# Three engines instead of two for the scale and shift of six norms, and a new order of the retention layer on one Trainium2 core

## The reference, cut to what matters

```
def rms_norm(x, g):
    y = xf * lax.rsqrt(jnp.mean(xf * xf, axis=-1, keepdims=True) + EPS)
    return y * g
def modulate(h, shift, scale):
    return h * (1 + scale) + shift
```

```
pv, q, k, v, g = split(h @ w_in)          # 512, 256, 256, 512, 512 wide
q, k = rope(q), rope(k)                   # a rotation inside each pair of channels
o = retention_bidir(q, k, v) with decays  # 4 heads: (q k^T * decay) v, both directions
y_r = rms_norm(o, gn_g) * silu(g)         # per head
y_p = multiscale_pool(pv)                 # windowed mean minus value, @ pool_w, * pool_scale
y = concat(y_p, y_r) @ w_out
```

## Time and profile before

| | us |
|---|---|
| median of three runs | 2321.37 |
| profiled execution, its device time | 2323.1 |
| span of that execution, first to last instruction | 2321.3 |
| PE busy | 2219.7 |
| DVE busy | 789.0 |
| ACT busy | 372.4 |
| POOL busy | 369.9 |

### The profile page before, as it was taken

How to read it: one execution, slowest core, us unless ns; L and a number is a source line. 1 busy time by engine, 2 the same in 40 slices (tenths; PEclk the granted TensorE clock), 3 DMA queues, 4 the chain that set the end, 5 groups by cost and what they waited for, 6 DMA issues and landing times.

```text
span 2321.3 us, 34149 instructions
## 1 busy us (share of the span) xinstructions
PE 2219.7 (96%) x11074; PEld 1272.1 (55%) x11075; DVE 789.0 (34%) x1709; ACT 372.4 (16%) x849; POOL 369.9 (16%) x2342
## 2 busy tenths in 40 slices
PE   6999999999999998999999899999899899999987
PEld 3464458888544677998888633333233233333323
DVE  1133655555560325884115321122121121111212
ACT  3222212111001312220224210010000010000001
POOL 0000020000001101000100033333233333333332
PEclk9999999999999999999999899999999999999999
DMA  9721342222584705557861399899999989989997
GB/s 381 248 74 55 104 133 91 91 91 82 174 269 146 236 1 182 164 165 260 283 211 61 146 382 422 354 423 422 383 397 422 422 357 422 422 358 422 422 422 289
DMA packets 196206, 602.76 MB, mean 260 GB/s; under 512 B 11042, under 2 KB 128034, under 8 KB 146850
## 3 DMA queue, kind: packets, MB, share of 16 engines
q1 hardware_dynamic: 193728, 599.04, 67.4%
q10 hardware_dynamic: 2402, 2.67, 0.4%
HBM read 600.62 MB, written 1.05 MB: 259 GB/s over the span
## 4 chain that ended last, share of the span: by engine, by line
PE 79%; DMA 12%; SPq 4%; DVE 2%; ACT 1%; POOL 1%; issue 1%; POOLq 0%; ACTq 0%; DVEq 0%
PE bank L371 52%; PE bank L964 26%; DMA wring<-in_w_gu 11%; SPq L2269 4%; DMA wring<-in_mod_w 1%; ACT big L1146 1%; POOL hT L2232 1%; DVE wring L1566 1%; PE bank L996 1%; ACT tmp L1146 0%; PE bank L989 0%; DVE big L1566 0%; DVE tmp L1566 0%; PE bank L677 0%; POOL xT L2259 0%
## 5 line engine op out<-in xcount | busy, mean ns | idle before, releaser
L964 PE MATMUL bank<-wring,big 128*64 128x512 f32 x3456 | 772.9, 596 | 41.1 <-DMA wring<-in_w_gu 32.7
L964 PEld LDWEIGHTS bank<-wring,big 128*64 128x64 f32 x3456 | 235.3, 137 | 529.4 <-issue 411.5
L371 PE MATMUL bank<-hT,wring 128*128 128x256 f32 (+2 forms) x1888 | 456.5, 396 | 8.3 <-POOL hT L2232 5.7
L371 PEld LDWEIGHTS bank<-hT,wring 128*128 128x128 f32 x1888 | 322.8, 193 | 125.1 <-issue 93.6
L371 PE MATMUL bank<-big,wring 128*128 128x256 f32 (+1 forms) x1096 | 344.7, 475 | 6.4 <-DVE big L1569 3.6
L2255 POOL COPY big<-hT 128x8 f32 x2240 | 306.7, 199 | 112.1 <-issue 112.1
L371 PEld LDWEIGHTS bank<-big,wring 128*128 128x128 f32 x1096 | 208.6, 191 | 138.9 <-issue 115.7
L371 PE MATMUL bank<-wring 128*128 128x256 f32 (+1 forms) x1408 | 245.9, 327 | 1.2 <-DVE wring L1566 1.1
L371 PEld LDWEIGHTS bank<-wring 128*128 128x128 f32 x1408 | 216.0, 191 | 20.3 <-DVE wring L1566 1.6
L1146 ACT ACTIVATE big<-bank 128x256 f32<-128x256 f32 (+3 forms) x239 | 89.5, 390 | 774.1 <-PE bank L989 385.4
L1569 DVE TENSOR_SCALAR big<-bank 128x512 f32<-128x512 f32 (+1 forms) x74 | 50.2, 678 | 447.2 <-PE bank L964 446.0
(11 more groups left out here) (169 smaller groups left out, 1240.5 us busy)
## 6 DMA issues: line engine op xcount, KB each, us to landing
wring<-in_w_gu SPq DMA_DIRECT2D x256, 1024.0 KB, 18.7
wring<-in_w_down SPq DMA_DIRECT2D x128, 1024.0 KB, 18.4
wring<-in_ffn_w_up SPq DMA_DIRECT2D x44, 1024.0 KB, 5.1
wring<-in_mod_w SPq DMA_DIRECT2D x24, 1024.0 KB, 15.5
wring<-in_mod_w SPq DMA_DIRECT2D x48, 512.0 KB, 4.4
wring<-in_ffn_w_down SPq DMA_DIRECT2D x16, 1024.0 KB, 5.6
wring<-in_w_ada SPq DMA_DIRECT2D x16, 1024.0 KB, 5.5
wring<-in_w_in SPq DMA_DIRECT2D x14, 1024.0 KB, 11.8
```

Source lines behind the costliest of these rows:

```text
L371: ins = pe.matmul(o, l, r, start=start, stop=stop, skip_group_check=True)
L964: ins = pe.matmul(o, l, r, start=start, stop=stop, skip_group_check=True)
```

## The change

It has two parts, which touch no weight, shape or result. First, the scale and shift of chunks 3 and 7 move from POOL to DVE in every norm: DVE scales chunks 0 to 3, does chunk 3's scale and shift, scales 4 to 7, and does chunk 7's (in norm 0, where the scale vector comes late, it does both behind the modulation). POOL keeps chunks 1 and 5. Second, the retention layer is reordered: PE does the rotations between the two value halves; the pooled part is projected ahead of the gates; DVE pools behind the first four decay multiplications; each head's sum of squares and its Ln and Exp follow one or two heads behind it; and DVE does the norms of heads 0 and 1 ahead of the four pool outputs, those of heads 2 and 3 behind them.

```diff
@@ PE, hwait
-                    if c % 2:
-                        pe.wait_ge(G("h_odd"), 4 * n + c // 2 + 1)
+                    if c % 2 == 0:
+                        pe.wait_ge(G("h_even"), 4 * n + c // 2 + 1)
+                    elif c % 4 == 1:
+                        pe.wait_ge(G("h_pool"), 2 * n + c // 4 + 1)
                     else:
-                        pe.wait_ge(G("h_even"), 4 * n + c // 2 + 1)
+                        pe.wait_ge(G("h_own"), 2 * n + c // 4 + 1)
...
@@ PE, retention
-            project_rows("v1", win, 1024, 2, range(4))
+            project_rows("v1", win, 1024, 2, range(4), (0,))
             for i in range(4):
                 key = ("rk", i) if i < 2 else ("rq", i - 2)
                 freed(pe, key)
                 bk, fl = claim(("rrot", i))
                 mm(bk[:, 0:S], rotm, RK[i][:, 0:S] if i < 2 else RQ[i - 2], True, True, fl)
+            project_rows("v1", win, 1024, 2, range(4), (1,))
...
+            def ret_stat(h):
+                stat(("ros", h), ones, [hT[:, h, 0:S]], lambda i: freed(pe, ("ro", h)))
+
+            for h in range(4):
+                ret_scores(2 * h)
+                ret_scores(2 * h + 1)
                 if h == 0:
+                    project([("rp", 0), ("rp", 1)], colsrc(win, 0), 2, S)
+                    project([("rp", 2), ("rp", 3)], colsrc(win, 256), 2, S)
+                if h == 1:
                     project([("rg", 0), ("rg", 1)], colsrc(win, 1536), 2, S)
                     project([("rg", 2), ("rg", 3)], colsrc(win, 1792), 2, S)
-                if h == 1:
-                    project([("rp", 0), ("rp", 1)], colsrc(win, 0), 2, S)
-                    project([("rp", 2), ("rp", 3)], colsrc(win, 256), 2, S)
                 if h:
                     ret_out(h - 1)
-            for h in range(4):
-                stat(("ros", h), ones, [hT[:, h, 0:S]], lambda i: freed(pe, ("ro", h)))
+                if h > 1:
+                    ret_stat(h - 2)
+            ret_out(3)
+            ret_stat(2)
...
                 mm(bk[:, 0:S], ws[:, P * g:P * g + P], RCAT[g], True, True, fl)
             done()
+            ret_stat(3)
             contract("wo1", od_w_out[0], RCAT, S,
...
@@ ACT, retention: rp copies ahead of rg's Silu, logs() behind it, then
+            for h in range(5):
+                if h < 4:
+                    bk = full(act, ("ro", h))
+                    A(RO[h], bk[:, 0:S], ACT.Copy)
+                    release(A(hT[:, h, 0:S], bk[:, 0:S], ACT.Square), ("ro", h))
+                if h:
+                    rstd(("ros", h - 1), RS[h - 1], P, S).then_inc(G("ro_rstd"), 1)
...
@@ DVE, norm
                     TT(hT[:, c, 0:T], xT[:, c, 0:T], tmp[:, 0, 0:T], MUL).then_inc(G("x_scaled"), 1)
+                    if n and c % 4 == 3:
+                        norm_affine(n, c)
+
+            def norm_affine(n, c):
+
+                m, part, T = NORM[n]
+                dve.wait_ge(G("gsc"), n + 1)
+                dve.wait_ge(G("x_scaled"), DC * n + c + 1)
+                for hf in range(T // S):
+                    h = hT[:, c, S * hf:S * hf + S]
+                    ins = TS(h, h, gsc[:, n, c, hf:hf + 1], modv[:, m, 8 * part + c, hf:hf + 1], MUL, ADD)
+                ins.then_inc(G("h_own"), 1)
...
@@ DVE, retention
+            for u in range(4):
+                ret_weigh(u)
+            dve.wait_ge(G("late_loaded"), 16)
+            for g, r in enumerate((1, 2, 4, 8)):
+                pool_rows(g, r)
+            for u in range(4, 8):
+                ret_weigh(u)
+            ret_norm(0)
+            ret_norm(1)
             for g in range(4):
                 bk = full(dve, ("pw", g))
                 release(TS(RCAT[g], bk[:, 0:S], V1("pscale", g), None, MUL), ("pw", g))
+            ret_norm(2)
+            ret_norm(3)
...
@@ POOL, norm_affine
-                for c in range(1, DC, 2):
+                for c in (1, 5):
```

More of the change, by code:

```diff
@@ L1356, in _ @@
                     decay(3)
+            for g in range(4):
+                bk = full(act, ("rp", g))
+                release(A(RCAT[g], bk[:, 0:S], ACT.Copy), ("rp", g))
             for j in range(4):
@@ L1360, in _ @@
                 release(A(RG[j], bk[:, 0:S], ACT.Silu), ("rg", j))
-            for g in range(4):
-                bk = full(act, ("rp", g))
-                release(A(RCAT[g], bk[:, 0:S], ACT.Copy), ("rp", g))
-            for h in range(4):
-                bk = full(act, ("ro", h))
-                A(RO[h], bk[:, 0:S], ACT.Copy)
-                release(A(hT[:, h, 0:S], bk[:, 0:S], ACT.Square), ("ro", h))
-            logs()
-            for h in range(4):
-                rstd(("ros", h), RS[h], P, S).then_inc(G("ro_rstd"), 1)
+            logs()
+            for h in range(5):
[5 more added lines that the diff above has]
+                    rstd(("ros", h - 1), RS[h - 1], P, S).then_inc(G("ro_rstd"), 1)
             norm(3, lambda c: freed(act, ("wo1", c)))
@@ L1879, in _, with ret_weigh @@
                 turn_pairs(x, EXPB[:, S * i:S * i + S], ("rrot", i)).then_inc(G("r_rope"), 1)
-            for u in range(8):
+            def ret_weigh(u):
                 bk = full(dve, ("ra", u))
@@ L1897, in _, with ret_norm @@
                 TT(RCAT[g], w_, RCAT[g], SUB).then_inc(G("pooled"), 1)
-            for h in range(4):
+            def ret_norm(h):
                 dve.wait_ge(G("ro_rstd"), h + 1)
```

17 lines of the change are left out of this document (8 added, 9 removed).

## The result

The changed kernel took 2306.93 us (median of 4 runs, 2305.96 to 2310.11) against 2321.4 us before (4 runs, 2318.51 to 2322.89): ratio 0.9942, 95% interval 0.9924 to 0.9959. Measured again on another chip it took 2308.53 us against 2323.15 (0.9940, 0.9926 to 0.9953). The forecast was 2309.8 us. The profiled execution took 2306.57 us, with a span of 2304.7 us.

What follows compares the result with a forecast made beforehand. PE, busy 96% of the span, was taken to bound the kernel; 1.1 (rotations) + 9.5 (retention's end) + 1.0 (norms) = 11.6 us off the 2321.37 us median gives 2309.8, own range 2306.5 to 2314, 8-in-10 range 2304.8 to 2316.5.

Steps and rivals of the forecast that it cites:

- The rotations, 1.1 us: Rotations between the value halves: old wait and half clock cost 6.8 us, new ones 5.7; 1.1 us gained, bounds -0.6 to 2.8.
- The wait for bank 0: Ahead of the second value half: PE waits 4.0 us until DVE's first rotation frees the bank, then 3.4 us at half clock.
- The end of the retention, 9.5 us: Last head statistics to output contraction: 7.5 us of waits and 2.0 us of half-clock loss go; 9.5 us, between 7 and 10.5.
- The last head's cover: Before the contraction: PE has 5.6 us of other work while the last head's norm takes 4.8 us, leaving 0.8 us.
- The norms, 1.0 us: All norms, with chunks 3 and 7 on DVE: 1.0 us gained in sum, from -2.5 to 2.
- Norm 2: PE waits for chunk 1, which stays on POOL; 0: Second-norm step: PE's wait for POOL's chunk 1 stays unchanged, so nothing is gained.
- norm 1: PE's 3.19 us wait for POOL's chunk 3 shortens, DVE's sums come later: 0.9 us gained, from 0 to 1.1.
- Norm 3: PE waits for DVE's `u2`, which two more DVE instructions delay: -0.5 us, from -0.8 to 0.
- Norm 5: With chunk 7 on DVE, the last chunk PE takes comes some 0.6 us earlier, from 0 to 0.8.
- The waits only move: Rival, chance 0.09: new waits and half clock replace the old; 4 us gained or less, 2317 to 2321 us.
- the rotations' wait does not come: Rival, chance 0.05: no new wait at the rotations, the whole 6.8 us go; 17 us gained, 2304 us.
- POOL is shut out: Rival, chance 0.04: at the norms DVE's longer run holds POOL back; 13 us lost against 10.6 gained, 2324 us.

Runs made afterwards that it cites:

- early table: Changed kernel with ScalarE's last decay table built behind the second, not the fourth, copy of the first value half: 2300.70 us, ratio to before 0.9906.
- retention alone: Kernel before with only the retention's part of the change, the scale-and-shift steps left as they were: 2312.97 us, ratio 0.9963.
- rotations back: Changed kernel with PE's rotations put back behind both value halves: 2308.99 us.
- pause behind 3 and 7: Kernel before with only a DVE wait for its own instruction added behind the scalings of chunks 3 and 7, not in norm 0: 2319.26 us, ratio 0.999.
- norms alone: Kernel before with only the move of scale and shift from POOL to DVE, retention left as it was: 2318.08 us, ratio 0.999.
- chunks swapped: Changed kernel with DVE doing scale and shift of chunks 1 and 5 and POOL those of 3 and 7: 2310.78 us, ratio 0.9945.

## Why the prediction was right, and where it was not

*The rotations, 1.1 us.* Measured 1.22. The wait for bank 0 came where it was said, 3.96 us for 4.0, with one stretch of half clock; the early table shows that the lateness of DVE's last decay sum is its cause. The 3.4 us of half clock came in six of the seven traces with this wait, but the reason given for it (matmuls that fill 128 rows against scores that fill 64) does not hold: behind waits of some 3 us ahead of 128-row products at norm 1 the clock was at half for 6.8 us in two traces (retention alone, rotations back), and behind the old wait ahead of the scores for only 3.4 us in one (pause behind 3 and 7, which is why that row of the table has −1.64). The length was a good guess.

*The end of the retention, 9.5 us.* Measured 9.71, in every run that has the edit whole. The pooling's place carries 8.2 of it. The last head's cover, 0.8 us in the sum, was 0.9.

*The norms, 1.0 us.* This is the step that failed. Norms 1 to 3 were to give 0.4 us and gave 4.6 (1.33 + 3.45 − 0.17); with norm 5 it is 5.1, far outside the term's own bounds (−2.5 to 2). "Norm 2: PE waits for chunk 1, which stays on POOL; 0" took POOL's 1.9 to 2.0 us for the length of an instruction beside DVE. They are for the most part waiting for DVE to leave an opening, and the change makes openings. So chunk 1 was ready 1.8 us earlier, and the wait left over (0.43 us) did not bring the clock down, which was worth 1.7 us more. At norm 1 the sum had the same error and left out the half clock behind the 3.19 us wait. PE's first products there came 2.5 us earlier (326.63 against 330.70, with the kernel 1.5 us ahead already), and the half clock that went was worth 1.7 us; waits of 1.14 us (POOL) and 1.11 us (DVE's sums) and the delays around them took some 2.9 us back. That the result, 1.33 us, lies near the 0.9 of the sum is luck. Norm 3 lost 0.17 us, not 0.5. Norm 5 gained 0.44 us where 0.6 was said: that is how far PE's products behind it (1313 to 1317.5 us of before) come out ahead in the changed kernel and in norms alone, against 0.00 in retention alone. The table doesn't show it, since in the changed kernel's traces, as in that of retention alone, 0.46 us are lost right behind: before, the clock was full from 1317.5 to 1320.9 us between two stretches at half, and there it is at half throughout.

*The rivals.* "The waits only move" did not happen, nor "the rotations' wait does not come". "POOL is shut out" was argued with the wrong premise, that more work on DVE is more lock-out. In the changed kernel's traces POOL's chunk 1 in norm 2 takes 2.13 us, not over 3; only in one trace (rotations back, norm 1) was an instruction held up for 3.19 us, over the 3 us that the prediction named as a sign of this for norm 2, and the stretch came out 2.2 us behind the other traces of that code. The page SBUF — State Buffer of the Trainium skill, section "Who interferes with whom", has next to the sentence that I leaned on another that bears on this kernel: a DVE instruction with two inputs in SBUF contends with a GpSimd instruction that reads it, while one with a single input, outside the two-port modes, does not. The traces agree for the first half: the scalings have two inputs and hold POOL up (0.98 to 3.19 us for 0.55). For the second they agree in the main: a POOL instruction begun beside the second affine step took 0.77 us and one wholly beside it 0.58 (chunks swapped), but there DVE's step took 0.64 us instead of 0.41, and beside such a step the one of 3.19 us began too. That the affine steps are outside the two-port modes is inferred from their pace: 0.33 us from start to start for 256 columns, against 0.60 for a scaling's 512 and 0.20 for 256 in the table instructions behind norm 2. If so, the change gives DVE more work only of the nearly harmless kind, and a pause. I had chosen the wrong sentence of the section.

*The sum.* In the profiled pair 16.5 us were gained, of which 11.6 were forecast: 4.1 more came from the norms, 0.3 from the retention and 1.3 from the chance half clock at norm 0, and 0.8 were lost elsewhere, 0.46 of them behind norm 5. The medians differ by 14.5 us. With the profile's own 1.3 us taken off, 15.2 us would have been expected of it. The range held because the retention's two terms, nine tenths of the sum, were read from waits that stand in the trace; the error of the norms was four times their term, and small beside those two. The first median, 2306.93 us, lies only 0.4 us above the lower end of the forecast's own range, 2306.5 to 2314.

## What to carry to other kernels

When an engine's instruction takes three times its own length beside another engine, ask whether it is slowed or waits for an opening, and look where it ends and what the other engine does there. Here moving two of eight steps, with a pause and a step of another kind in the row, gave 4.6 us at norms 1 to 3; the wait alone at the same two places gave 2.3, and a wait behind every scaling gave 0.9, since DVE's longer row cost norms 1 and 3 2.2 of the 3.1 us that norm 2 gained. So ask for an opening where the needed instruction is held up, and not everywhere. And when a moved step meets a new wait, follow it back to the last thing ahead of it in a queue: here a table built two copies earlier, on a ScalarE that stood waiting for PE between the copies (3.07 us each time), was worth 5.6 us, half as much as the retention's edit.

## What was not expected of the hardware

POOL's affine instruction (128x256) took 0.55 us alone, 1.89 and 2.02 beside an unbroken row of two-input DVE instructions, 0.98 where DVE paused behind each, 0.77 begun beside the second of two one-input instructions, 0.58 wholly beside it, and once 3.19. With 0.03 us between two scalings one POOL instruction got in, and the scaling behind it took 0.93 us instead of 0.68. What lets POOL in after 1.9 us where DVE does not pause, and what kept it out for 3.19, no run here shows.

The half clock behind a wait is not a fixed price. Behind PE waits of 2.19 us in norm 2 it came both times, behind 1.67 and 1.31 us it did not; behind the same 4 us wait at the rotations it was 3.4 us in six traces and 6.8 in one, behind the old wait there 6.8 us in four and 3.4 in one, and at norm 0 it was 0, 3.4 or 6.8 us between runs of the same code (0 and 3.4 for the changed kernel).
